# Down weights of the expert items issued from ScalarE's queue, between its rounds of Silu

## The reference

```python
def moe_swiglu(h, router, wg, wu, wd):
    ...
    top_vals, top_idx = lax.top_k(logits, TOP_K)          # 2 of 8 experts per token
    gates = jax.nn.softmax(top_vals, axis=-1)
    ...
    for e in range(N_EXPERTS):
        out = out + dense_gate[:, e:e + 1] * swiglu(ht, wg[e], wu[e], wd[e])

def swiglu(h, wg, wu, wd):
    return jnp.einsum('...f,fd->...d', jax.nn.silu(h @ wg) * (h @ wu), wd)
```

## Time and profile before

| | us |
|---|---|
| median of 3 runs | 1380.44 |
| lowest and highest | 1378.47, 1381.91 |
| the profiled execution's own time | 1387.19 |
| its span, first to last instruction | 1385.4 |
| items 0 to 7 of the experts, in the trace | about 406 to 1112 |

### The profile page before, as it was taken

How to read it: one execution, slowest core, us unless ns; L and a number is a source line. 1 busy time by engine, 2 the same in 40 slices (tenths; PEclk the granted TensorE clock), 3 DMA queues, 4 the chain that set the end, 5 groups by cost and what they waited for, 6 DMA issues and landing times.

```text
span 1385.4 us, 32504 instructions
## 1 busy us (share of the span) xinstructions
PE 1354.6 (98%) x14828; PEld 939.3 (68%) x14828; DVE 510.1 (37%) x829; ACT 382.6 (28%) x519; POOL 85.0 (6%) x142
## 2 busy tenths in 40 slices
PE   6999999999999999999999999999989999999998
PEld 6879999888775544545445454454536678798896
DVE  6976454459762101001010010100101265647655
ACT  5665434345530000000000000000000246645643
POOL 3400000025010000000000000000012110000000
PEclk9999999999989999999999999999999999999999
DMA  9568885446559999999999999999999944343251
GB/s 327 183 231 290 287 275 196 135 158 207 206 213 401 404 410 409 414 411 411 414 404 414 412 410 414 407 414 410 410 362 379 345 168 134 120 143 131 93 185 59
DMA packets 122743, 408.43 MB, mean 295 GB/s; under 512 B 7282, under 2 KB 35810, under 8 KB 122608
## 3 DMA queue, kind: packets, MB, share of 16 engines
q1 hardware_dynamic: 114144, 390.88, 74.2%
q0 software_dynamic: 5600, 12.58, 2.8%
q10 hardware_dynamic: 2864, 2.88, 0.6%
HBM read 398.09 MB, written 16.52 MB: 299 GB/s over the span
## 4 chain that ended last, share of the span: by engine, by line
PE 88%; DVE 8%; ACT 2%; issue 1%; DMA 0%; SPq 0%; DVEq 0%; ACTq 0%
PE ps L2681 50%; PE ps L503 7%; PE ps L505 6%; PE ps L504 6%; DVE yT L2017 3%; PE ps L1186 2%; PE ps L1188 2%; PE ps L1187 2%; DVE low L493 2%; PE ps L2372 1%; PE ps L2334 1%; PE ps L1395 1%; PE ps L1393 1%; PE ps L1394 1%; DVE yT L2014 1%
## 5 line engine op out<-in xcount | busy, mean ns | idle before, releaser
L2681 PE MATMUL ps<-ering,xe 128*32 128x384 f32 (+1 forms) x6144 | 462.7, 461 | 7.3 <-issue 7.3
L2681 PEld LDWEIGHTS ps<-ering,xe 128*32 128x32 f32 x6144 | 214.4, 110 | 252.7 <-issue 138.7
L2681 PE MATMUL ps<-ering,eT 128*32 128x256 f32 x4224 | 233.0, 379 | 0.4
L2193 DVE TENSOR_TENSOR eh<-eh,ps 128x384 f32<-128x384 f32 (+1 forms) x48 | 22.1, 517 | 546.7 <-PE ps L2681 531.6
L2681 PEld LDWEIGHTS ps<-ering,eT 128*32 128x32 f32 x4224 | 141.5, 110 | 88.5 <-issue 2.6
L493 DVE TENSOR_TENSOR low<-raw,high 128x2048 fp32r<-128x2048 f32 (+3 forms) x48 | 128.7, 2683 | 61.6 <-ACT high L488 60.4
L488 ACT ACTIVATE high<-raw 128x2048 fp32r<-128x2048 f32 (+3 forms) x47 | 105.5, 2244 | 91.8 <-PE ps L505 76.1
L503 PE MATMUL ps<-high,xT_hi 128*128 128x352 f32 (+1 forms) x368 | 128.2, 348 | 1.2 <-DVE xT_lo L2099 1.2
L505 PE MATMUL ps<-high,xT_lo 128*128 128x352 f32 (+1 forms) x368 | 127.1, 345 | 0.0
L504 PE MATMUL ps<-low,xT_hi 128*128 128x352 f32 (+1 forms) x368 | 126.8, 345 | 0.0
L1872 ACT ACTIVATE eh<-ps 128x384 f32<-128x384 f32 (+1 forms) x48 | 18.8, 465 | 346.4 <-PE ps L2681 346.4
(11 more groups left out here) (437 smaller groups left out, 1634.1 us busy)
## 6 DMA issues: line engine op xcount, KB each, us to landing
ering<-in_moe_wd SPq DMA_DIRECT2D x48, 1536.0 KB, 13.9
ering<-in_moe_wg SPq DMA_DIRECT2D x32, 1536.0 KB, 13.1
ering<-in_moe_wu SPq DMA_DIRECT2D x32, 1536.0 KB, 16.3
ering<-in_moe_wg SPq DMA_DIRECT2D x32, 1280.0 KB, 12.5
ering<-in_moe_wu SPq DMA_DIRECT2D x32, 1280.0 KB, 11.0
rawb<-in_w_in SPq DMA_DIRECT2D x25, 1024.0 KB, 5.1
raw<-in_w_in SPq DMA_DIRECT2D x16, 1024.0 KB, 9.4
ering<-in_moe_wd SPq DMA_DIRECT2D x16, 1024.0 KB, 14.2
```

The source lines that it names most:

```text
L2681: mm = nc.tensor.matmul(out_of(rows), tokens, columns_of(s), start=begins, stop=ends, skip_group_check=True)
```

## The change

SP's loops over the chunks end at 16. The eight down chunks of every item are issued by ScalarE: 16, 17 and 18 between its two rounds of Silu, 19 to 23 after the second. The waits before each load are the same as before, now on ScalarE. Slots, tiles and the order on TensorE stay.

```diff
             def load_item(i, e, last=False):
-                for j in range(FFN_CHUNKS):
+                for j in range(16):
                     if j == 12 and not last:
                         load_tokens(i)
                     sp.wait_ge(w_used, chunk(i, j - ESLOTS + 1))
                     load_expert(sp, e, j)
...
-            def item(i):
+            def load_down(i, e, j):
+                act.wait_ge(w_used, chunk(i, j - ESLOTS + 1))
+                load_expert(act, e, j)
+
+            def item(i, e):
                 if not isinstance(i, int):
                     finish(i)
                 for piece in range(2):
+                    if piece:
+                        for j in range(16, 19):
+                            load_down(i, e, j)
                     act.wait_ge(w_used, chunk(i, 8 * piece + 3) + 1)
                     for t in range(TOKS):
                         nc.scalar.activation(eh[piece][:, t, 0:WIDE[piece]], ps[:, t, 0:WIDE[piece]], ACT.Silu).then_inc(esilu_made, 1)
+                for j in range(19, FFN_CHUNKS):
+                    load_down(i, e, j)
```

More of the change, by code:

```diff
@@ L1893, in _ @@
                                      ps[:, GATHER_BANKS[p], 0:2 * CAP].rearrange("p (t n) -> p t n", t=2), ACT.Copy).then_inc(g0_hi, 1)
-            item(0)
+            item(0, 0)
             with act.Fori(1, NE - 1) as i:
-                item(i)
+                item(i, i)
             act.wait_ge(routed, 1)
@@ L1901, in _ @@
                     with act.If(i < last):
-                        item(i)
-            item(last)
+                        e = act.value_load(plan[0:1, bass.ds(i - (NE - 1), 1)], min_val=0, max_val=NE - 1)
+                        item(i, e)
+            item(last, NE - 1)
             second_scalar(act, last + 1, prepare, norm_std, xt_high, finish)
```

## The result

| | before | after |
|---|---|---|
| median | 1380.38 us (8 runs, 1378.47 to 1381.91) | 1383.55 us (8 runs, 1382.53 to 1385.64) |
| ratio | | 1.0024, 95% interval 1.0016 to 1.0033 |
| the profiled execution, its span | 1387.19, 1385.4 | 1383.58, 1381.7 |

The changed kernel is 3.2 us slower, inside the 0.3% that the prediction calls no change, and by its interval not zero.

The account below looks back on a forecast made before the run. TensorE was taken as the bound, with DMA loads just ahead. Stalls of 4.3 us, partly taken back by faster mixed queues, gave +3 us on the 1380.44 us median: 1383.5 us, range 1378.5 to 1391.5.

Parts of the forecast that it names:

- The bound and the reserve: Items 1 to 6: TensorE full at 86.24 us an item; chunk 23's loads keep ahead, by 8.8 us at the smallest.
- What was costed at nothing: SP's 24 us of issues removed and ScalarE's 24 us added both lie in waiting time: 0 us, bounded by 0 and 0.4.
- The order of the loads: Ends of items 3 to 6: next item's packets delay chunk 23 by 1.5 times the down backlog B; stalls sum to 4.3 us.
- near equal numbers: Sign at each change of item: packets of queues 1 and 10 in near equal numbers, as the engines alternate packet by packet.
- The mixing gain: Some 35 us per item with both queues busy: 1.4% more DMA rate, 0.5 us an item, taking back part of the stalls.
- The mirror case: ScalarE's chunk 16 beside SP's up chunks 13 to 15: chunk 15 of item 6 lags 22.6 us, just in time; no term.
- The clock: Short waits of TensorE in items 3 to 6 should not lower the clock; otherwise each would cost about 2.9 us.
- The handover: End of item 7: rawb loads pass beside the last down chunks; ScalarE has 4.85 us to spare before the output copy; 0 us.
- (a): Whole kernel: nothing visible happens, since TensorE is full or the reserve is larger; 1380.5 to 1382 us; chance 0.23.
- (b): Stretches with both queues: two weight streams disturb each other, losing 1% (over 6 us) to 3% (1391 us); chance 0.15.
- (c): Before chunk 23: stalls as computed, or first packets of SP's load after 1 us; 4.3 to 6 us, 1384.7 to 1386.5; chance 0.20.
- (d): After item 6: the 6.05 us pause at the branch and slow clock behind it shrink; faster, 1375 us; chance 0.05.

Follow-up runs that it names:

- half rows: Changed kernel with each gate load of chunks 0 to 3 issued as two DMAs of half the columns: 1385.00 us, ratio 1.0035 to the kernel before.
- later start: Changed kernel with SP's load of chunk 0 of items 1 to 7 waiting for chunk 17 instead of 16 of the item before: 1388.76 us, ratio 1.0018.
- half rows before: Kernel before, all loads on SP, with each gate load of chunks 0 to 3 issued as two DMAs of half the columns: 1384.92 us, ratio 1.0035.
- the long packets: Changed kernel with down chunks 20 to 23 read in pieces of 8 or 12 KB: 1386.24 us, ratio 0.9998; same reading in the kernel before: 1386.59 us, 0.9997.

## Why the prediction was right, step by step

**The bound and the reserve.** Right. TensorE's period of an item, 86.23 us, stayed wherever it didn't wait, and the reserve of 8.8 us for chunk 23 was what the change used up. It was not the smallest: by the prediction's own figures chunk 15 of item 6 had 22.75 less 15.2, or 7.55 us.

**What was costed at nothing.** ScalarE's issues take 0.374 to 0.390 us and delay neither Silus nor copies; half of them taken back (chunks 19 to 23) removes the loss, the other half taken back doesn't. SP's time saved buys nothing.

**The order of the loads.** The mechanism, its place and its size were right: waits before chunk 23, only there, 3.8 us longer in all against 4.3 forecast. How they fall was not: 1.1 us in each of items 4, 5 and 6, where 1.1, 0.35, 1.3 and 1.5 in items 3 to 6 were forecast; and the lag in item 1 was 17.4 us, not 20. Two parts of the reasoning were off. The packets of SP's load flow 3.5 us after issue, not 2 us: in the window from 813.2 to 816.6 queue 1 moved nothing. The trace of before could have told it: the first packets of ScalarE's seven ys stores, beside SP's busy queue, come 3.5 to 3.6 us after issue. With 3.5 us, B is 1.5 us smaller and every lag 2.25 us shorter: 17.6, 19.6, 25.4, 27.3 us in items 1 to 4, against 17.4, 21.8, 24.0 and 27.7 measured. Item 3 is then inside its reserve, as it was, and the stalls begin in item 4. The sum hardly moves: by the prediction's rule for what gives way it is 4.1 us instead of 4.3. Second, "near equal numbers" of packets was wrong as a sign: 920 to 329, nearly three to one. The time at which the 16 engines count up a chunk's semaphore tells why (trace of the changed kernel, item 4, us; a chunk has landed with the last):

```
chunk 22: 815.1 815.1 815.2 815.3 815.3 815.4 815.6 816.2   827.5 827.8 827.9 828.6 829.1 829.3 829.4 830.1
chunk 23: 818.3 818.4 818.5 818.8 819.0 819.1 819.5 821.1   833.8 834.1 834.2 834.9 835.6 835.7 836.5 836.9
```

Eight engines run ahead of the other eight; when the next item's load comes, the eight in front are all but done with the down chunks and serve queue 1 alone. Only the eight behind have both. The counts fit: in 16 us a pair of packets of 0.395 us passes 41 times on each of eight engines, 324 of each kind, and 68 gate packets of 0.235 us on each of the others, 545; that is 324 and 869, and the trace has 307 of 4096 bytes and 871 of 6144. And chunks 22 and 23 land 6.3 and 6.8 us after the one ahead of them: 16 packets an engine in 6.3 us is 0.39 us a packet, which is one packet of 4.1 KB and one of 6.1 KB together (0.16 and 0.235 us in the trace). On the engines that set the landing the queues do alternate one to one.

The trace shows this packet by packet. It names no engine, but a packet starts 2 to 5 ns before the one ahead of it on its engine ends, and where just one fits, the pair is known. From 803 to 812 us, down loads alone, all 587 such pairs are of queue 10. From 819 to 835 us 234 pairs go from queue 10 to queue 1, 232 from queue 1 to queue 10, 389 from queue 1 to queue 1 (the eight engines in front), and none from queue 10 to queue 10: no engine served two rows of down weights one after the other. In the store's case before, from 586.5 to 592 us, 193 and 196 pairs change queue, 3 stay on queue 1 and none on queue 10.

The rule that the prediction named from the Trainium skill (DMA: Bandwidth & Descriptors, "Queues, rings and completion order") thus holds for each engine, and can't be read off the sum over 16. One thing differs: what the page calls a packet is a group of typically 9 to 17 descriptors, drained whole before the engine changes queue, while here the change comes after every single row of 4 or 6 KB, which is one packet of the profile; the measurement decides.

**The mixing gain.** This is the term that was wrong. With both queues at work the rate was 413 to 415 GB/s at the ends of items 3, 4 and 6, but the kernel before, on one queue, moved 414 GB/s from 730.5 to 747 us as well, where the changed kernel moved 415 on two; and the earlier trace rows themselves have 416 on one queue from 1004 to 1012 us. Up to the first stall, from 495 to 836 us, it is 410 GB/s in the changed kernel and 411 before. There was no gain to take back part of the stalls. So that +3 us hit 3.2 is in part luck: without the gain the same working gives 4.3 us, or 4.1 with the 3.5 us put right, where the traces show 3.8. The interval of the measurement, 2.2 to 4.6 us, holds all of these and can't tell them apart.

**The mirror case.** "No term" was right for the changed kernel, where chunk 15 of item 6 had a lag of 17.9 us (forecast: 22.6 less 5) and kept 4.5 us, but the margin is thin: with slightly more load or a later start the wait moves there (half rows, later start).

**The clock.** Waits of 1.1 us each did not lower it: 1.00 from 495 to 1013 us. Nor did those of 1.7 to 1.9 us before chunk 15 (half rows, later start). But behind the wait of 2.35 us (chunks 19 to 23 on ScalarE) and that of 3.0 us (half rows before) it was at 0.50, which cost 1.5 and 2.3 us beyond the wait. The right forecast thus rests on the stalls being short ones, several instead of one.

**The handover.** Costed at 0, and 0 it was: from TensorE's next product to the end it is 272.7 us before and 272.8 after. But the cover named, 4.85 us, belonged to the delays of item 7 in that trace. In the trace of the changed kernel ScalarE's output copy begins with 0.48 us of idle time before it:

```profile
1108.02 0.60 ACT L1890 ACTIVATE eo<-ps 128x512 f32<-128x512 f32 x1 [0.48 <-PE ps L2691]
```

With the halved gate loads of the control this cover was gone, and with the clock behind the wait it cost 5.0 us.

**The rivals.** (a), nothing visible, 0 to 1.6 us, is excluded by the interval, which starts at 2.2. (b), streams that disturb each other, is excluded by the rate and by the long packets. (c), the stalls without the gain, 4.3 to 6 us, is not excluded at its lower end, and in its mechanism it is what the traces show. (d), a shorter pause at the branch: it is 6.01 us now, 6.05 before. **The profile's own time:** that it lay 6.75 us above the median was taken as a property of profiling to be carried over. It goes with the delays of item 7, and most likely with the chip; carrying over only the difference of 3 us was right all the same.

## What to carry to other kernels

Here a second DMA queue added no bandwidth to a part that was already full (410 GB/s against 411), but it took away the order: where two queues have work each engine serves a packet of each in turn (in 855 pairs of packets queue 10 never comes twice), and the queue with the longer packets gets the larger share, wanted or not. Before splitting one stream over two issuers, take the reserve of the chunk that is last in its queue (time wanted less time landed) and the backlog B ahead of it when the other queue wakes; it will be late by about B times the ratio of the packet sizes, the other queue's over its own (here within 2.2 us in items 1 to 4). If two queues must be, give the urgent one the long packets, as the run with rows of 8 and 12 KB did.

## What the runs showed of the hardware that was not expected

- The 16 engines don't keep step: on one and the same load the eight faster ones finish 7 to 8 us before the slowest with one queue (item 4 of the kernel before, chunk 23: first increments at 818.8 to 819.9, last 824.1 to 826.8 us), and 14 to 19 us before it with two (chunks 22 and 23 above). The lag that grows by 1.2 us an item is that of the slower eight: in the kernel before the eighth increment of chunk 23 comes 9.4 us after issue in item 1 and 9.3 in item 6, the last 11.9 and 17.9. Why they are slower the runs don't show.
- The first packet of a load comes 3.5 us after its issue while the other queue is busy, 1.0 us when the engines are idle (issues at 359.14 and 410.28 us of the kernel before).
- With chunks 0 to 3 in twice the number of packets, and all else the same, an issue holds its issuer for up to 5.4 us per DMA.
- Packets of 8 and 12 KB moved as fast as those of 4 KB or slightly faster: in the kernel before, chunk 23 of item 6 landed 15.6 us after issue with them and 17.9 without (on different chips).
- TensorE's short delays beside GpSimd's gathers, some 5 us in the last item, go with the chip in the runs here: present in all three traces of the second chip and in that of the kernel before, absent in all four of the first. Their cause is open.
